# Expert products in another order, odd mixer with pooled columns first and a split output projection, retention's output groups behind its norm

## The reference, cut to what matters

```
def _expert_ffn(xb, w_gu, b_gu, w_down, b_down):
    gu = xb @ w_gu + b_gu
    gate, up = gu[:, :D_EXPERT], gu[:, D_EXPERT:]
    gate = jnp.minimum(gate, SWIGLU_LIMIT)
    up = jnp.clip(up, -SWIGLU_LIMIT, SWIGLU_LIMIT)
    glu = gate * jax.nn.sigmoid(SWIGLU_ALPHA * gate)
    return ((up + 1.0) * glu) @ w_down + b_down
...
    yb = retention(pad_left(hd(bq, B_HEADS)), pad_left(hd(bk, B_HEADS)),
                   pad_left(hd(bv, B_HEADS)))[:, META_PAD:]
    yb = rms_norm(yb).astype(h.dtype).reshape(B, L, -1) * jax.nn.silu(bg)
    return jnp.concatenate([ya, yb], axis=-1) @ w_out
...
def odd_mixer(h, w_in, c_qn, c_kn, c_sinks, d_mix, d_scale, w_out):
    cq, ck, cv, dx = split_cols(h @ w_in, ODD_SIZES)
    cq = rms_norm(hd(cq, C_HEADS), c_qn)
    ck = rms_norm(hd(ck, C_KV_HEADS), c_kn)
    yc = swa_sinks(pad_left(cq), pad_left(ck), pad_left(hd(cv, C_KV_HEADS)), c_sinks)
    yd = pool_mixer(dx, d_mix, d_scale)
    return jnp.concatenate([yc, yd], axis=-1) @ w_out
```

## Time and profile before

| | us |
|---|---|
| runs before (3) | 3123.46, 3124.87, 3125.57 |
| median | 3124.87 |
| profiled execution | 3121.96 |
| its span | 3120.2 |
| TensorE busy in the span | 2958.1 (95%) |
| VectorE, ScalarE busy | 821.1, 368.5 |

### The profile page before, as it was taken

One profiled execution on the slowest core, in us unless ns is written; L12 is line 12 of the kernel. 1 busy time (PEld: TensorE's weight loads), 2 busy tenths in 40 slices (PEclk: granted clock), 3 DMA queues, 4 the chain that ended last, 5 costly groups with the idle time before them and its releaser, 6 DMA issues.

```text
span 3120.2 us, 35482 instructions
## 1 busy us (share of the span) xinstructions
PE 2958.1 (95%) x14711; PEld 1939.7 (62%) x14712; DVE 821.1 (26%) x1908; ACT 368.5 (12%) x781; POOL 28.3 (1%) x56
## 2 busy tenths in 40 slices
PE   8989889989999999999989999999999999989999
PEld 6967678843333333333337887676788888756888
DVE  2536341222222222222222101542211111133210
ACT  1122230110000000000011000122000000012000
POOL 0000000000000000000000000000000000000000
PEclk9999999999999999999999999999999999987999
DMA  5122234459999999999983334221343334321340
GB/s 193 57 91 82 88 115 170 192 193 418 422 424 422 421 425 422 424 422 421 424 353 129 141 135 146 108 82 62 113 157 135 135 135 148 143 81 55 139 158 14
DMA packets 49530, 654.90 MB, mean 210 GB/s; under 512 B 5840, under 2 KB 8032, under 8 KB 10224
## 3 DMA queue, kind: packets, MB, share of 16 engines
q1 hardware_dynamic: 45248, 642.90, 51.6%
q0 software_dynamic: 3136, 9.38, 0.9%
q10 hardware_dynamic: 1040, 1.05, 0.1%
HBM read 652.26 MB, written 1.05 MB: 209 GB/s over the span
## 4 chain that ended last, share of the span: by engine, by line
PE 92%; DVE 4%; ACT 2%; issue 1%; DMA 1%; POOL 0%; PEldq 0%; DVEq 0%; PEld 0%; SPq 0%; ACTq 0%; POOLq 0%
PE bank L305 77%; PE bank L2073 2%; PE bank L1090 2%; PE bank L2045 2%; PE bank L2447 1%; DVE expert_x_slots L2177 1%; PE bank L2460 1%; PE bank L2051 1%; ACT expert_y_slots L2119 1%; PE bank L2303 1%; PE bank L2468 1%; PE bank L1342 1%; PE bank L736 0%; PE bank L726 0%; PE bank L2061 0%
## 5 line engine op out<-in xcount | busy, mean ns | idle before, releaser
L305 PE MATMUL bank<-ffn_x_gained,weight_ring 128*128 128x272 f32 (+1 forms) x2816 | 640.8, 390 | 9.3 <-DVE ffn_x_gained L2320 9.3
L305 PEld LDWEIGHTS bank<-ffn_x_gained,weight_ring 128*128 128x128 f32 x2816 | 536.4, 191 | 112.4 <-DVE ffn_x_gained L2320 11.0
L305 PE MATMUL bank<-weight_ring,expert_x_slots_t 128*64 128x512 f32 x2048 | 456.1, 598 | 0.0
L305 PE MATMUL bank<-x,first_weight_ring 128*128 128x256 f32 x1376 | 323.7, 392 | 28.9 <-DMA first_weight_ring<-weight_stream 12.8
L305 PEld LDWEIGHTS bank<-weight_ring,expert_x_slots_t 128*64 128x64 f32 x2048 | 141.9, 137 | 311.4 <-issue 311.4
L305 PE MATMUL bank<-ffn_h,weight_ring 128*128 128x272 f32 (+1 forms) x1408 | 322.0, 389 | 2.1 <-DVE ffn_up L2399 2.1
L305 PEld LDWEIGHTS bank<-x,first_weight_ring 128*128 128x128 f32 x1376 | 266.6, 196 | 73.1 <-issue 24.0
L305 PEld LDWEIGHTS bank<-ffn_h,weight_ring 128*128 128x128 f32 x1408 | 267.2, 190 | 54.0 <-DVE ffn_up L2399 3.8
L305 PE MATMUL bank<-weight_ring,expert_hidden_slots_t 128*64 128x512 f32 x1024 | 226.8, 595 | 0.0
L305 PE MATMUL bank<-even_hn,weight_ring 128*128 128x272 f32 x656 | 162.8, 405 | 4.4 <-DVE even_hn L2337 4.4
L2182 DVE TENSOR_TENSOR moe_rows<-moe_rows,bank 128x512 f32<-128x512 f32 x128 | 79.3, 681 | 330.9 <-PE bank L2073 330.9
(11 more groups left out here) (580 smaller groups left out, 2293.6 us busy)
## 6 DMA issues: line engine op xcount, KB each, us to landing
weight_ring<-weight_stream SPq DMA_DIRECT2D x276, 2048.0 KB, 9.1
first_weight_ring<-weight_stream SPq DMA_DIRECT2D x30, 2048.0 KB, 7.7
x<-x_t SPq DMA_DIRECT2D x1, 1024.0 KB, 5.8
out_t<-x ACTq DMA_DIRECT2D x1, 1024.0 KB, 4.7
c_ret_ret_q<-const_ret_q POOLq DMA_DIRECT2D x1, 544.0 KB, 5.2
c_ret_ret_k<-const_ret_k POOLq DMA_DIRECT2D x1, 544.0 KB, 5.7
c_odd_pool_inv<-const_pool_inv POOLq DMA_DIRECT2D x1, 544.0 KB, 3.8
c_hgrn_hgrn_levels<-const_hgrn_levels POOLq DMA_DIRECT2D x1, 512.0 KB, 3.6
```

Of the source, the lines that this page charges most:

```text
L305: ins = K.nc.tensor.matmul(out, lhsT, rhs, start=start, stop=stop)
```

## The change

Four parts.
- In `few` the spread turns go to bank 0 (after a wait that gate was read), the gather is cut in two halves by token block with the hidden turns between them, and the turns of the gathered tokens go behind the down products, into bank 3; ScalarE's copy of them goes behind that of the output.
- In retention the groups of heads 0 to 4 stay in the head loop; the last three stand behind the gathers. VectorE makes the variance, one group's add, the reciprocal, then the other two adds.
- In the odd mixer the column order is pooled, keys, queries, in two banks, and gathers and mixes stand between the later columns. VectorE makes the window steps as columns arrive.
- The odd output projection is cut in two: the half that takes the pooled part (weight tiles 4 to 7) runs beside the attention turns, 2 tiles a turn, and VectorE adds a group every second turn; the half that takes the attention's output follows without the barrier. The weight stream is reordered to match.

```diff
+BESIDE_HEADS = 5
...
+    per_out("od_w_in_2", (0,), kx, range(768, 1280, P))
+    per_out("od_ck", None, kx, [0, P])
     per_out("od_w_in_2", (0,), kx, range(0, 512, P))
...
-    per_out("od_w_out_2", (0,), kx, range(0, D, P))
+    per_out("od_w_out_2", (0,), range(4, 8), range(0, D, P))
+    per_out("od_w_out_2", (0,), range(4), range(0, D, P))
...
             def few(pe):
...
                 pe.wait_ge(*spread_ready.take())
+                pe.wait_ge(*gate_read.take())
                 for b in range(2):
-                    nc.tensor.transpose(bank[2][:, b * P:(b + 1) * P], spread[:, b, :, :].rearrange("p a s -> p (a s)"), eye)
-                gather_next(pe)
+                    nc.tensor.transpose(bank[0][:, b * P:(b + 1) * P], spread[:, b, :, :].rearrange("p a s -> p (a s)"), eye)
+                gather_next(pe, 0)
                 pe.wait_ge(*h_ready.take())
                 for j in range(4):
                     ins = nc.tensor.transpose(bank[5][:, j * P:(j + 1) * P], h[:, 0, j * P:(j + 1) * P], eye)
                 ins.then_inc(*ht_ready.post())
-                turn_next(pe)
+                gather_next(pe, 1)
                 pe.wait_ge(*ht_sb.take())
                 few_linear(pe, bank[2], ht_few, None, y_ready)
+                turn_next(pe, 3)
                 pe.wait_ge(*ys_sb.take())
...
-                copy_next(act)
                 act.wait_ge(*y_ready.take())
                 act.activation(ys[:, :], bank[2][:, :], ACT.Copy).then_inc(*ys_sb.post())
+                copy_next(act, 3)
...
+            def first_part(j):
+                if j:
+                    pe.wait_ge(*a_free.take())
+                for k in range(4):
+                    matmul(K, bank[7][:, 0:T], K.weights.take(pe), y[:, k, :], k == 0, k == 3, a_ready if k == 3 else None)
...
+                if h < BESIDE_HEADS:
+                    first_part(h)
...
             heads.gather(pe, 7)
+            for j in range(BESIDE_HEADS, 8):
+                first_part(j)
...
+            heads.variance(dve)
+            first_part(BESIDE_HEADS)
+            heads.invert(dve)
+            for j in range(BESIDE_HEADS + 1, 8):
+                first_part(j)
...
+class OddBeside:
...
+    def tensor(self, pe, n):
+        K = self.K
+        j, half = divmod(n, 2)
+        if half == 0 and j >= 2:
+            pe.wait_ge(*self.free.take())
+        for k in (2 * half, 2 * half + 1):
+            matmul(K, K.bank[6 + j % 2][:, 0:T1], K.weights.take(pe), self.y[:, 4 + k, META:T2], k == 0, k == 3, self.ready if k == 3 else None)
...
+    def vector(self, dve, n):
+        K = self.K
+        j, half = divmod(n, 2)
+        if half:
+            dve.wait_ge(*self.ready.take())
+            dve.tensor_tensor(out=K.x[:, j, META:T2], in0=K.x[:, j, META:T2], in1=K.bank[6 + j % 2][:, 0:T1], op=ALU.add).then_inc(*self.free.post())
...
+            for j in range(10):
+                columns.tensor(pe, 6 + j % 2, first=K.rms.hn_ready if j == 0 else None)
+                if j == 4:
                     pe.wait_ge(K.small_loaded, loads)
...
+                if j > 4:
+                    heads.gather(pe, j - 5)
+                if j > 5:
+                    mix(j - 6)
+            for k in range(DT):
+                w = K.weights.take(pe)
+                for b, (t0, tn) in enumerate(Q3):
+                    matmul(K, bank[v_banks[b]][0:tn, 0:P], hn[:, k, t0:t0 + tn], w, k == 0, k == DT - 1, v_ready if k == DT - 1 else None)
+                if k == 1:
+                    heads.gather(pe, 5)
+            pe.wait_ge(*mix_free.take(2))
             for j in range(6):
                 heads.spread(pe, j)
...
-        end_stage(K)
-        out_projection(K, "od", y, 8, META)
+            beside.vector(dve, 15)
+        out_projection(K, "od", y, 4, META)
```

More of the change, by code:

```diff
@@ L2887, in _ @@
                 ins.then_inc(*o_ready.post())
-                if h:
-                    pe.wait_ge(*a_free.take())
-                for k in range(4):
-                    matmul(K, bank[7][:, 0:T], K.weights.take(pe), y[:, k, :], k == 0, k == 3, a_ready if k == 3 else None)
+                if h < BESIDE_HEADS:
+                    first_part(h)
                 if h == 0:
@@ L2921, in masked, with first_part @@
                 ins.then_inc(*s_sb.post())
+            def first_part(j):
+                dve.wait_ge(*a_ready.take())
+                dve.tensor_tensor(out=K.x[:, j, :], in0=K.x[:, j, :], in1=bank[7][:, 0:T], op=ALU.add).then_inc(*a_free.post())
             masked(0)
@@ L2929, in _ @@
                 dve.tensor_tensor(out=bg[:, h, :], in0=bg[:, h, :], in1=bank[6][:, 0:T], op=ALU.mult).then_inc(*o_free.post())
-                dve.wait_ge(*a_ready.take())
-                dve.tensor_tensor(out=K.x[:, h, :], in0=K.x[:, h, :], in1=bank[7][:, 0:T], op=ALU.add).then_inc(*a_free.post())
+                if h < BESIDE_HEADS:
+                    first_part(h)
+            heads.variance(dve)
[3 more added lines that the diff above has]
+                first_part(j)
             dve.wait_ge(*a_free.posted())
-            heads.vector(dve)
             for j in range(8):
@@ L2988, in odd_mixer, with mix @@
                          lambda h, kt: cv[:, kt, 64 * (h // 4):64 * (h // 4) + 64],
[L2989 removed]
+                         lambda qt: con["swa_mask"][:, qt * T:(qt + 1) * T], y, sink=sinks, queries=Q_OUT, beside=beside)
         @block.tensor
         def _(pe):
[L2993 to L3000 removed]
+            def mix(j):
+                pe.wait_ge(*pool_ready.take())
+                if j >= 2:
+                    pe.wait_ge(*mix_free.take())
+                nc.tensor.matmul(bank[j % 2][:, 0:T], dmix[:, j, :], pooled[:, j, :], start=True, stop=True).then_inc(*mix_ready.post())
+            for j in range(10):
+                columns.tensor(pe, 6 + j % 2, first=K.rms.hn_ready if j == 0 else None)
+                if j == 4:
+                    pe.wait_ge(K.small_loaded, loads)
+                if j > 4:
[9 more added lines that the diff above has]
+            pe.wait_ge(*mix_free.take(2))
             for j in range(6):
                 heads.spread(pe, j)
[L3003 to L3006 removed]
+            columns.until(pe, 10)
+            pe.wait_ge(*v_free.take(3))
             pe.wait_ge(*qk_ready.take())
```

103 lines of the change are left out of this document (53 added, 50 removed).

## The result

The changed kernel takes 3082.39 us (median of four runs, 3080.90 to 3084.21) against 3124.16 for the kernel before beside it. The ratio is 0.9866, with a 95% interval of 0.9852 to 0.9880: 41.8 us faster, where 53 was forecast. The predicted 3072 is 10 us too low; the range of 3059 to 3097 holds the result.

The account below looks back on a forecast made before the run. TensorE, 92% of the chain that ended last, was taken as the bound. Terms -25.5 - 2.6 - 2.6 - 14.5 - 0.5 - 6 - 1.5 = -53 us gave 3072 against 3124.87; range 3059 to 3097.

Parts of the forecast that it names:

- Experts: Expert loop: down products start 0.82 us earlier per expert, less 0.7 for the weight ring; -25.5 us.
- Rival C: Expert loop: the weight ring starves the experts at 4.95 us a load, 3081 us; chance 0.12.
- Rival D: Expert loop: the new body is fetched anew each round, slower, 3246 us if ending every expert; chance 0.02.
- Retention: Retention's tail: three output groups moved into the pause behind the gathers, -1.7 us, and -0.9 for the clock.
- The clock's term: Retention's tail: the clock falls again but later, around the spreads; -0.9 us (0 to -3.5).
- Odd mixer up to attention: Odd mixer before its attention: mixes move between the columns and waits go; -2.6 us (0 to -4).
- Projection: Odd output projection after attention: groups of 8 products instead of 16, starting at full clock; -16.0 us.
- Attention: Odd attention: full clock returns after three or four turns, 55.5 us, -6; with the barrier gone -6.5.
- rival B: Odd attention: clock stays at half through most of it; never back 3099 us, back midway 3086; chance 0.2.
- rival A: The main forecast, with odd attention's clock back within the first six turns: 3062 to 3084 us; chance 0.63.

Follow-up runs that it names:

- one_in_wait: Changed kernel with one pair of weight tiles in the pause behind the first scores and one in each of turns 0 to 14: 3081.47 us, ratio 0.9864.
- od_shift: Changed kernel with four products of 272 columns added ahead of the odd mixer's fourth column tile, attention unchanged: 3065.19 us, ratio 0.9808.
- re_tail: Changed kernel with retention's last output groups in banks of their own and the last group in two halves between its spreads: 3067.89 us, ratio 0.9819.
- early: Changed kernel with spreads among the values' last products, four weight-tile pairs ahead of odd attention, twelve in three of four turns: 3074.57 us, ratio 0.9851.

## Why the prediction was right and wrong

**Experts, right.** The mechanism and the order in an expert came as worked out, and so did the two rates: TensorE's period 28.86 (forecast 28.94), the ring's 29.36 (29.4). TensorE saved 0.90 and not 0.82 per expert. That made the shortage 0.50 instead of 0.46, and the reserve lasted for the third to the 25th expert instead of to the end: 23 x 0.50 = 11.5 us, where 13 had been reckoned. So the waits began at 1401 and not near 1600, and they stood in the middle of the up products, where the working had looked at a load wanted in the down products. Both errors are small and of opposite sign: -24.3 for -25.5. Rival C (starving at 4.95 us a load) is out: six loads took 29.36, 4.89 each. That is 429 GB/s; the Trainium skill's 425 (DMA: Bandwidth & Descriptors, Bandwidth), by which the term would have been about -18, is a little low here, and its ceiling of 435 was not reached. Rival D is out as well: one stall of 5.36 us after the first expert, none later.

**Retention, right, one term small.** Behind the gathers, 4.4 more was forecast up to the first spread: (2154.16 - 2145.75) - (2181.53 - 2177.51) = 4.39. Ahead of them the loop gave 5.5 and not 6.1, since the last head now waits 0.49. The clock's term was the mis-sized one: the fall moved behind the spreads, which gave the whole 2.1 us of theirs, forecast 0.9.

**Odd mixer up to attention, right.** -3.8 for -2.6, inside its bounds. The stretch ahead of the values' products grew by 0.4 (2770.90 - 2726.08 = 44.82 before, 2741.77 - 2696.57 = 45.20 after), where about 1.7 had been reckoned; 0.55 of the difference is the last gather, which now stands among the values' products. The rest, 0.8, was not traced.

**Projection, right.** -16.4 for -16.0: groups of eight products, at full clock from the start.

**Attention, wrong.** This is the step that failed: "I take a return after three or four turns". The two levels between which it chose were right: two turns 9.94 us at half clock (forecast 9.8) and 5.84 at full (5.7). Only the time of the return was off: after ten turns, so +8.7 instead of -6.5. That is what rival B says, "back midway 3086", to which 0.2 was given; A's condition, a return within the first six turns, failed. The result, 3082, still lies among A's times, 3062 to 3084, since the other stretches gave 3.3 us more than forecast, 2.2 of them from the loop's earlier start, which is no work of the change. That the range held the result is owed to its width and to this luck, not to this term. The argument for A was that at half clock the products beside leave no gap. They leave none, and `one_in_wait` shows that no gap is not enough. The other argument, the nearness to the even attention and to retention, was the better one and was read too generously: the rounds that held 1.00 had 2.0 and 3.9 us of wide products in one piece, this one 0.9.

But B was not simply the truth either. With `od_shift` and `re_tail` the unchanged attention had the clock back in the second and the third turn, and the kernels took 3065 and 3068 us: rival A's time. Which of the two comes out was decided by 2 us of work 45 or 600 us upstream. No row that the prediction read tells that. The forecast should have had two peaks, near 3063 and near 3082, and 3072 lies between them, where neither outcome of this attention is.

**Open.** What sets the moment is not settled. The runs show that a shift of the same work changes when the clock falls and returns, and that a kernel mostly comes out alike in its runs (within 4 us for the changed one, though 3072 to 3081 for `early`). They don't show why the start of the expert loop, which differs by up to 3.9 us between the traces, mostly leaves that unmoved: it is 656.65 in the changed kernel and 659.40 in `one_in_wait`, and both are at half clock for 55 us. Each kernel has one trace, so how far the start moves between executions of one kernel isn't shown. The changed kernel was not run again beside `od_shift`; the two are compared through the kernel before, which took 3124.16 and 3125.07 us. Nor was it tried whether a block of eight holds at every moment: it did in the three kernels that had it.

## What to carry to other kernels

Where TensorE does short or narrow products in a dependent loop, give it a block of wide products (eight of 256 columns here) right after the place at which the clock falls, and leave no round without some: in the three kernels with such a block that was worth 18 to 20 us in a stage of 128. It is a thing to try and not a rule, for in `od_shift` 1.9 us of work upstream was worth nearly as much, with four products in a turn as in the changed kernel. Before a gain or a loss of that size is put down to an edit, look at the granted clock of every stretch behind it, for a small shift upstream can move it. And when two resources are within 2% of each other, work out when the reserve between them ends: it paid for 25 of 32 experts here.

## What was not expected of the hardware

- The granted clock stayed at 0.50 for 55 us while TensorE was busy 53.14 of 53.50 us, with transposes, 64-row scores, 64-column values and four 256-column weight products in a turn.
- Adding 1.9 us of products made the kernel 18 us faster.
- The stall of TensorE after the first round of the loop was 5.36 us with the ring loading 2 MiB pieces (up to 6.41 in the other traces) and 3.22 with 1 MiB pieces, and the products behind it took 18.84 and 17.79.
- The clock fell in spreads with 16-row operands and hardly a pause: in the changed kernel TensorE was busy for 7.73 of the 8.00 us ahead of the fall.
